# Two parts of VectorE's hand-written order moved in the mixers of a hybrid decoder trunk

## What is computed

```python
h = rmsnorm(x, ln1_g[layer])
proj = h @ w_in[layer]
a_u, a_b, a_c, s_u, q, k, v, qi, ki, wi, gates = split_columns(proj)
y_a = short_conv_mixer(a_u, a_b, a_c, conv_w) @ w_out_a      # a_b * conv3(a_c * a_u)
y_b = s5_mixer(s_u, ...) @ w_out_b                           # diagonal complex state space
y_c = dsa_mixer(q, k, v, qi, ki, wi, ...) @ w_out_c          # sparse attention
x = x + (g0 * y_a + g1 * y_b + g2 * y_c) @ w_o

# inside dsa_mixer, for each of the two blocks of 128 queries:
rel = relu(einsum('bthd,bsd->bths', qi_block, ki))
score = where(causal, einsum('bths,bth->bts', rel, wi), -inf)
_, sel = top_k(score, 64)                                    # the "best keys"
p = softmax(q_block @ k[sel] * scale);  out = p @ v[sel]
```

## Time and profile before

| | us |
|---|---|
| median of 3 runs | 1691.57 (1690.58 to 1691.79) |
| profiled execution, its own time | 1690.0 |
| its span | 1688.1 |
| TensorE busy | 1634.7 (97%) |
| VectorE busy | 1377.7 (82%) |
| ScalarE busy | 1072.0 (64%) |
| GpSimd busy | 459.3 (27%) |

### The profile page before, as it was taken

The page is one execution under the profiler, slowest core; times in us unless marked ns, Lnnn a source line. Parts: engine busy times, 40 slices in busy tenths (PEclk is TensorE's granted clock), DMA queues, the critical chain, the costliest instruction groups (busy, mean ns, idle before and its releaser), DMA issues.

```text
span 1688.1 us, 24269 instructions
## 1 busy us (share of the span) xinstructions
PE 1634.7 (97%) x8944; PEld 1389.7 (82%) x8944; DVE 1377.7 (82%) x1140; ACT 1072.0 (64%) x896; POOL 459.3 (27%) x541
## 2 busy tenths in 40 slices
PE   6889998999999999999999999999999999999998
PEld 5787888989989788878888888888888888888886
DVE  6999775555569977688888888888888988888888
ACT  6345455444454455477777777777777777777775
POOL 8996801999233532225000000000000000000200
PEclk9899999999999999999999999999999999999999
DMA  8343556556554554569999999999999999999994
GB/s 316 119 158 124 175 177 206 175 180 209 167 164 137 151 161 172 166 252 393 389 383 383 372 378 391 363 383 387 370 388 382 370 386 378 376 383 372 391 395 190
DMA packets 212459, 481.57 MB, mean 285 GB/s; under 512 B 7936, under 2 KB 32640, under 8 KB 212144
## 3 DMA queue, kind: packets, MB, share of 16 engines
q1 hardware_dynamic: 207456, 463.34, 76.6%
q0 software_dynamic: 4512, 16.78, 2.7%
q10 hardware_dynamic: 432, 0.65, 0.1%
HBM read 473.40 MB, written 7.34 MB: 285 GB/s over the span
## 4 chain that ended last, share of the span: by engine, by line
PE 67%; DVE 2%; ACT 1%; issue 0%; DVEq 0%; ACTq 0%
PE ps L649 20%; PE ps L651 20%; PE ps L650 20%; PE ps L1257 1%; PE ps L673 1%; PE ps L675 1%; PE ps L674 1%; DVE w_lo L281 1%; PE ps L848 0%; PE ps L1333 0%; PE ps L1210 0%; ACT w_hi L276 0%; PE ps L1314 0%; DVE keybias L2081 0%; DVE keybias L2079 0%
## 5 line engine op out<-in xcount | busy, mean ns | idle before, releaser
L281 DVE TENSOR_TENSOR w_lo<-raw,w_hi 128x2048 fp32r<-128x2048 f32 (+1 forms) x439 | 1017.3, 2320 | 229.5 <-ACT w_hi L276 227.9
L276 ACT ACTIVATE w_hi<-raw 128x2048 fp32r<-128x2048 f32 (+1 forms) x439 | 841.2, 1917 | 418.7 <-PE ps L651 331.2
L649 PE MATMUL ps<-w_hi,xg_hi 128*128 128x512 f32 x896 | 354.5, 396 | 1.2 <-DVE w_lo L281 1.2
L651 PE MATMUL ps<-w_hi,xg_lo 128*128 128x512 f32 x896 | 349.6, 390 | 0.0
L650 PE MATMUL ps<-w_lo,xg_hi 128*128 128x512 f32 x896 | 349.1, 390 | 0.0
L649 PE MATMUL ps<-w_hi,hidT_hi 128*128 128x512 f32 x520 | 204.2, 393 | 1.9 <-DVE hidT_lo L2372 1.8
L651 PE MATMUL ps<-w_hi,hidT_lo 128*128 128x512 f32 x520 | 203.2, 391 | 0.0
L650 PE MATMUL ps<-w_lo,hidT_hi 128*128 128x512 f32 x520 | 203.1, 391 | 0.0
L651 PEld LDWEIGHTS ps<-w_hi,xg_lo 128*128 128x128 f32 x896 | 168.1, 188 | 35.9
L649 PEld LDWEIGHTS ps<-w_hi,xg_hi 128*128 128x128 f32 x896 | 168.3, 188 | 35.4 <-DVE w_lo L281 1.6
L650 PEld LDWEIGHTS ps<-w_lo,xg_hi 128*128 128x128 f32 x896 | 168.5, 188 | 33.3
(11 more groups left out here) (411 smaller groups left out, 2379.5 us busy)
## 6 DMA issues: line engine op xcount, KB each, us to landing
raw<-moe_w SPq DMA_DIRECT2D x336, 1024.0 KB, 6.6
raw<-w_in SPq DMA_DIRECT2D x44, 1024.0 KB, 5.6
raw<-ffn_w SPq DMA_DIRECT2D x33, 1024.0 KB, 5.4
raw<-w_o SPq DMA_DIRECT2D x8, 1024.0 KB, 5.1
raw<-w_out_a SPq DMA_DIRECT2D x4, 1024.0 KB, 5.2
raw<-w_out_c SPq DMA_DIRECT2D x4, 1024.0 KB, 6.1
raw<-w_out_b SPq DMA_DIRECT2D x4, 1024.0 KB, 5.1
raw<-w_in SPq DMA_DIRECT2D x4, 904.0 KB, 7.7
```

Of the source, the lines that this page charges most:

```text
L276: act.activation(w_hi[:, n % SPLIT, 0:width], raw[:, n % RAW, 0:width], ACT.Copy).then_inc(hi_done, 1)
L281: dve.tensor_tensor(w_lo[:, n % SPLIT, 0:width], raw[:, n % RAW, 0:width], w_hi[:, n % SPLIT, 0:width].bitcast(F32), ALU.subtract).then_in ...
L649: pe.matmul(dst, x_hi, hi, start=first, stop=False, skip_group_check=True)
L651: return pe.matmul(dst, x_lo, hi, start=False, stop=last, skip_group_check=True)
```

## The change

In both mixers VectorE makes the low part of chunk 7, the eighth, straight after that of chunk 6 and ahead of `score(layer, 1)`. All eight rounds for block 0 then stand together. Block 1's eight rounds stand together too, between `turn_q(2)` and `invert_sums(layer, 1)`. No instruction is added or taken away.

```diff
                 chunk(6)
+                chunk(7)
                 score(layer, 1)
                 clear_second()
-                best(layer, 0, 0, 4)
-                chunk(7)
-                best(layer, 0, 4, 8)
+                best(layer, 0, 0, 8)
                 choose(0)
                 bias_of_choice(0)
                 chunk(8)
                 chunk(9)
-                best(layer, 1, 0, 4)
                 shift(layer, 0)
                 clear_edge()
                 chunk(10)
-                best(layer, 1, 4, 8)
                 invert_sums(layer, 0)
...
                 conv_output(layer)
                 turn_q(2)
+                best(layer, 1, 0, 8)
                 invert_sums(layer, 1)
                 conv_lo()
```

## The result

The changed kernel took 1700.84 us (median of 5 runs, 1700.42 to 1706.53), the kernel before 1691.44 us on the same chip: a ratio of 1.0065, 95% interval 1.0055 to 1.0076 (it is taken over all runs; the two medians alone give 1.0056). The loss of 9.4 us between the medians is what was forecast (9.3), and so is the time (1700.8). The profiled execution was the longest of the five, 1706.53 us, so a part of what its trace shows is not in the median; what the change touches is therefore read within each mixer.

A forecast was written before the change was run, and what follows sets the result against it. VectorE, late in the mixers, was taken as the bound, showing as TensorE's waits. Mixers' +5.45 and +3.85 us on the profiled 1690.0 gave 1699.3; with the median 1.6 above that execution, 1700.8 was named, range 1694.5 to 1705.

The forecast's parts named there:

- Part 1, mixer 1: First mixer, chunk 7 moved ahead: wait goes at conv_u(1), returns at conv_c(0) as 4.5 us; gain 1.9 us at shift(1).
- The 0.9 us added for the scores: First mixer, chunk 8's low part: 0.9 us later because block 1's scores run later beside GpSimd's rotary; bounds 0 and 2.2.
- the slow start: TensorE behind a long wait runs at half clock for a while; taken as 1.4 us lost each time in the first mixer.
- the sum's 0.4 and 0.5: First mixer: gains from the wait at turn_probs(0) going (0.4 us) and shift(1) following its logits closely (0.5 us).
- Part 1, mixer 2: Second mixer, chunk 7 moved ahead: its wait goes, nearly none at chunk 8; gain 3.5 us, bounds 2.5 and 3.7.
- Part 2: Block 1's rounds behind turn_q(2): 7.35 us per mixer, less the earlier gain; +5.45 us first mixer, +3.85 us second.
- edit as meant: Rival: chunk 7's waits go in full in both mixers, rounds covered behind turn_q(2); 1681 us, chance 0.03.
- The sum: Both mixers together: 5.45 + 3.85 = 9.3 us slower than the kernel before.
- rival 1: Block 1's scores in both mixers escape GpSimd's rotary: 11.2 us off VectorE, 1689.7, chance 0.05; partial case around 1693, 0.09.
- rival 2: New TensorE waits at chunk 8, turn_probs(1) and chunk 17 add up with unabsorbed slow starts; about 1706 us, chance 0.10.

The follow-up runs named there:

- awake: Changed kernel plus 18 unread multiplications on TensorE ahead of conv_c(0) in the first mixer, filling its wait for chunk 8; 1702.16 us, ratio 1.0062.
- sums_first: Changed kernel with invert_sums(1) ahead of block 1's rounds instead of behind them; 1708.55 us, ratio 1.0099.
- after_again: The changed kernel once more, unaltered, for a second profile; 1701.82 us, ratio 1.0070.
- gaps: Changed kernel with block 1's eight rounds put into VectorE's idle stretches after invert_sums(0), chunk 11's low part and conv_input; 1690.48 us, ratio 0.9994.
- act_scale: Kernel before, with ScalarE instead of VectorE making the first scaled score of each block; 1690.38 us, ratio 0.9995.
- spare_late: Changed kernel plus eight redundant MAX8 per mixer on VectorE behind turn_q(2), ahead of block 1's rounds; 1708.18 us, ratio 1.0099.
- both spare runs: Changed kernel plus eight redundant MAX8 per mixer on VectorE: after invert_sums(0), 1701.92 us, or behind turn_q(2), 1708.18 us.
- gaps_scale: Block 1's rounds in VectorE's idle stretches and ScalarE making each block's first scaled score, together; 1691.42 us, ratio 1.0004.

## Why the prediction was right

**Part 1, mixer 1: right in kind, the gain too large.** Chunk 7 was ready in time, conv_u(1) did not wait, and the wait came back at conv_c(0): 4.53 us at 81.02, forecast 4.5 at 81.2. The 0.9 us added for the scores was 0.5: they took 7.1 us instead of 6.4 and chunk 7's low part some 0.6 more, and block 0's rounds and choice behind them won 0.9 back. That was all in the first two instructions of the choice (L2112 and L2113), which took 0.82 and 0.77 us before, from 74.11 on, and 0.33 and 0.28 us now. It was not the rotary, which had ended at 69.5 before; GpSimd was making the state space's powers by then (L311), and why the two got faster was not tested. By the rule of the Trainium skill (SBUF — State Buffer, Who interferes with whom) the addition would have been at its upper side, up to 2.2; the measured 0.5 doesn't bear that out. The scores and chunk 7's low part came near it, with 1.4 us more; what the choice won back was not in that sum.

The term that was mis-sized is the slow start. I took 1.4 us from the one behind the wait of 5.51 us. Behind the 4.53 us the clock stayed at 0.50 to 0.51 for 5.8 us (to 86.8), and at half the speed that is 2.7 us more than at full speed by the awake run: there the clock was up, conv_c(0) began 1.1 us later and turn_probs(0) came 1.5 us earlier, 2.7 in all. With 81.02 + 2.7 = 83.7 conv_c(0) gained nothing over the 83.6 of before, where I had 1.0. What was left is the sum's 0.4 and 0.5, and shift(1) came 110.12 - 109.14 = 0.98 us earlier, not 1.9. The keys_only run bears that out: there chunk 7 was not moved, and shift(1) still came 0.71 us earlier (109.41). But 2.7 us is no better a constant than 1.4. From conv_c(0) to turn_probs(0) awake took 17.3 us and the changed kernel 19.9; sums_first, behind the same wait, took 18.7, so it lost only 1.4 us, and after_again and gaps took 19.5, a loss of 2.2. On chunk 7, behind waits of 5.5 and 5.4 us, keys_only lost 1.5 us and act_scale 2.7. The forecast had taken one draw for a fixed price; and where the draw was good, the table held shift(1) at 1.4 us.

**Part 1, mixer 2: right.** No wait at either chunk, and a gain at shift(1) of 3.9 us (49.5 us after L893, at 563.34, where it was 53.4 us after it, at 556.29), forecast 3.5; in after_again it is 3.5.

**Part 2: right, to a few hundredths.** The rounds took 7.34 us (7.35). Nothing covers them: 7.34 - 0.98 = 6.4 is how much later invert_sums(1) came. The rival "edit as meant" needed cover there and found none; spare_late shows it with other instructions, at 3.65 and 3.96 us of delay to turn_probs(1) for 3.6 us of work. turn_probs(1) waited 3.8 and 6.9 us (foretold: 4 to 7 in both, about 5 in the first). In mixer 1 the loss is 6.65 us (forecast 5.45, bounds 4.0 to 6.8): 0.9 of the 1.2 too much is the missing gain, 0.3 came behind invert_sums(1). In mixer 2 it is 3.35 and 4.4 (forecast 3.85, bounds 3.6 to 4.9), or 4.9 and 4.4 from block 0's index scores.

**The sum** is 10.0 us in one profile and 11.1 in the other, against 9.3; the medians give 9.4 and 11.3. So the 0.04 us between forecast and median is luck: the first mixer was 1.2 us dearer than I had it, and the changed kernel alone moved by 1.0 us between its two medians (1700.84 and 1701.82).

**The rivals.** The scores did not escape the rotary: 7.1 and, in mixer 2, 6.4 us instead of 6.4 and 8.6. The second mixer's 2.2 us are like the partial case of rival 1, and the term had taken in a little over 1 us of them; but it is no escape, since the rotary goes on to 530.1 there, 3 us beyond the scores. Of rival 2 there was one thing, in the first mixer only: the slow start behind the wait at chunk 8 was not absorbed, and it took 1.3 us more than the 1.4 that the forecast had counted. The edit as meant (1681) is refuted by c7_only, which keeps all of the edit's gain and none of its cost and stands at 1692.4.

## What to carry to other kernels

An instruction on an in-order engine has no price of its own: the same sixteen (eight in each mixer) cost 0.1 to 1.1 us between them at one place and 6.4 to 7.3 at another 40 us later. Before work is moved, look for the engine's idle stretches in the trace, and ask whether any is left where the work stands now once it is gone: here 6.7 us of idle time opened on VectorE just where the rounds had stood. It is their going that opened it: keys_only, which moves only the rounds, has 5.8 us of it in the first mixer and another 1.1 ahead of shift(0), and c7_only, which moves only chunk 7, has none there (timeline of VectorE, keys_only):
```profile
91.78 2.54 DVE L281 TENSOR_TENSOR w_lo<-raw,w_hi 128x2048 fp32r<-128x2048 f32 x1 [3.78 <-ACT w_hi L276]
...
95.53 1.22 DVE L2243 TENSOR_TENSOR uv<-uv,ps 128x1024 f32<-128x1024 f32 x1 [1.22 <-PE ps L675]
```
The rounds had stood where they cost next to nothing.

A wait that is removed shows the next one. Where the engine waited for is late and has no idle time, the order of its work only chooses where the waiting is done, and each place at which the other engine stands for some us can have a slow start of its own; take the price of that slow start as a span, 1.4 to 2.7 us here, and not from one row.

## What was not expected of the hardware

- **The slow stretch behind a wait has no fixed length.** After 5.51 us of idleness it lasted 3.0 us, after 4.53 us 5.8 us. Nor does it go with the length of the wait: behind the wait of 4.5 us at conv_c(0) it lasted 5.8 us in c7_only and the first profile of the changed kernel, 4.5 to 4.9 in after_again, gaps and both spare runs, and 3.1 in sums_first; behind 5.4 us at conv_u(1) in act_scale it lasted 6. A wait of 2.1 us at conv_u(0) left the clock at 1.00 in the gaps run and at 0.72, on the mean of the next 6.2 us, in the awake run: 1.5 us, from nothing that the edits changed there.
```profile
60.10:66.30 6.20, 6.04 (x50) 1.00 0.82 255
```
(windows of TensorE, gaps; awake's row for the same stretch stands above). And of sums_first, behind its wait of 4.52 us:
```profile
81.10:84.20 3.10, 3.05 (x14) 0.50 0.66 161
```
- **A pattern outside the edit.** Between the mixers TensorE waits for the low part of the dense layer's activations. The waits list has one such wait, of 1.8 us, in the profiles of before, keys_only, gaps, gaps_scale and both spare runs, and this in the first of the changed kernel (columns: us in total, times, longest):
```profile
PE ps L649 <- DVE hidT_lo L2370: 5.3, 4, 1.8
```
The same 5.2 to 5.3 us stand in after_again, c7_only, sums_first, awake and act_scale. No property of the edits that I could find divides the two groups, and no run tried to. It goes with the 2.9 us that hid act_scale's gain in mixer 2, and it accounts for 2.8 of the 6.6 us by which the profiled execution of the changed kernel is longer outside its mixers; 1.5 more lie ahead of the second mixer's scores and 2.3 behind that mixer. These stay open.
